# A decoder step's attention: inverse sums turned one place later, the sample's fourth key group, new keys and row turns moved in the plan

## The chip, the core and the metric

The kernel runs on one core of one Trainium2 chip. The metric is the device time of one execution in microseconds (us), the median of several runs. The engines are TensorE (PE; its weight loads are PEld), VectorE (DVE), ScalarE (ACT), GpSimd (POOL) and SyncE (SP), which here issues the DMAs.

## What is computed

One layer of a decoder for a prompt group (1024 tokens, 1 sequence) and a sample group (8 sequences of 8 new tokens, each with 2048 cached keys in 16 pages). The layer is a half-step feed-forward block, three branches on the normed input (sparse attention, a gated recurrence, cross-attention into 256 memory tokens), their gated merge, and a second half-step feed-forward block. The part that matters here:

```python
def sparse_core(q, k_sel, v_sel, valid):
    s = jnp.einsum("bthd,btkhd->bthk", q, k_sel, preferred_element_type=jnp.float32) * (DH_ATT ** -0.5)
    s = jnp.where(valid[:, :, None, :], s, -jnp.inf)
    p = jax.nn.softmax(s, axis=-1).astype(v_sel.dtype)
    o = jnp.einsum("bthk,btkhd->bthd", p, v_sel)

def mem_attend(qm, mk, mv):
    s = jnp.einsum("bthd,bmhd->bthm", qm, mk, preferred_element_type=jnp.float32) * (DH_MEM ** -0.5)
    p = jax.nn.softmax(s, axis=-1).astype(mv.dtype)
    o = jnp.einsum("bthm,bmhd->bthd", p, mv)
```

## The kernel before

The kernel first runs feed-forward 1 and the input projections, then head norms (`keys_and_heads`), then `attention`, whose last steps run into `merge`, then feed-forward 2. Only `attention_plan` (L2802) is touched. It returns a list of entries in one order, and `on_pe`, `on_act` and `on_dve` (L3141, L3322, L3380) each walk that list and issue their share of every entry. So the list is the program order of all three engines. An engine's instruction waits on semaphores, and all that is queued behind it on that engine waits too.

The prompt's work is cut into 48 **doubles**: for each of 4 head pairs, 8 doubles of attention (query blocks of 128 rows in the order 0, 7, 1, 6, 2, 5, 3, 4; a query block i sees 128(i+1) keys, two heads at a time) and 4 of memory attention (two query blocks, one head). The entries of a double d are

- `scores` (L3160): TensorE forms the scores into banks 0 to 3; VectorE reduces them to negative maxima (L3406, or L3410 and L3412 for memory). Scores of d wait until those of d-1 are read: by VectorE's reduction for attention, by ScalarE's exponentials for memory (`scores_read`, L2983).
- `exp` (L3332): ScalarE takes two exponentials with row sums.
- `turn` (L3188): TensorE transposes the probabilities, up to 4 blocks a turn, and ScalarE or VectorE copies the bank out (`evict`, L2995; the even turns of the plan go to ScalarE, the odd ones to VectorE).
- `invert` (L3413): VectorE takes the reciprocals of the sums and spreads them (L3422, memory L3425).
- `inverse` (L3217): TensorE transposes these (L3221) once VectorE has spread them; they are copied out (L3013).
- `values` (L3194): TensorE multiplies the turned probabilities with the values (L3210, L3214) and VectorE scales the product by the turned inverse (L3432).

In step d the order is scores(d), a first place for the sample, values(d-2), a second place, turn(d-1), invert(d-1), exp(d), a third place, and last inverse(d-1). Right behind the scores of steps 8, 20 and 32 ScalarE copies the next head pair's queries (L3310), and behind those of steps 9, 21 and 33 its keys (L3313); there VectorE takes the low parts of both (L3372, L3374).

The sample's work fills the three places. Each of the 8 samples takes six steps: `sc` 0 to 3 are the scores against four groups of four key pages (TensorE L3236 and L3246, copied out by ScalarE at L3355), `sc` 4 those against the 8 new keys, `smax` VectorE's row maximum over all 2056 columns (L3437), `soft` ScalarE's exponential (L3360), `msc` memory scores, `pt` 0 to 4 the turns of the probabilities (L3261, L3263), `pv` the product with the 16 value pages (L3281), `mpt` and `mpv` the same for memory, `ot` and `mot` the turns of the results. All matmuls of the sample go through bank 5, one after another, each behind the copy of the one before (`freed5`).

Turns take the least recently used of banks 4, 7, 1 and 3; in a **wide** step (d mod 12 in 1, 3, 5, 7, over 512 keys) of 4 and 7 alone, as the scores need 1 and 3.

SyncE loads the pages in its own order: three key slots, so that a sample's group 3 goes into the slot of its group 0 and waits for `sc` 0, and the next sample's group 2 waits for `sc` 3 (L3087). The loads of the value pages wait for `pv` and `mpv` of the sample before (L3101).

Behind double 47, `merge` entries 0 to 4 bring in the first pieces of the merge; entries 3 and 4 give TensorE a branch product each (L3590), which waits for GpSimd's low part of the first weight (L3585).

Of the kernel before, what the change touches and what calls it, by code (L numbers as in the profile page):

```python
# [2801 lines left out]
def attention_plan():  # L2802

    doubles = []
    for hp in range(H // 2):  # L2810
        doubles += [("att", i, 2 * hp) for i in (0, 7, 1, 6, 2, 5, 3, 4)] + [("mem", 2 * m, hp) for m in range(4)]
    slots = [
        ([], [], [("sc", 0)]),
        ([("sc", 1)], [], [("sc", 2)]),
        ([("sc", 3)], [], [("sc", 4), ("smax",)]),
        ([], [], [("soft",), ("msc",)]),
        ([("pt", 0), ("pt", 1), ("pt", 2)], [("pt", 3), ("pt", 4)], [("pv",), ("mpt",)]),
        ([("mpv",)], [("ot",)], [("mot",)]),
    ]
    plan = []  # L2820
    turns = 0

    def add(step, *entry):
        nonlocal turns
        turn = None
        if entry[0] in ("turn", "inverse", "pt", "mpt", "ot", "mot"):
            turn = turns
            turns += 1
        plan.append((entry, turn, step))

    def sample(d, place):
        if d < n:
            for e in slots[d % 6][place]:
                add(d, e[0], d // 6, *e[1:])

    n = len(doubles)
    add(0, "queries", 0)
    add(0, "keys", 0)
    for d in range(n + 2):
        if d < n:  # L2840
            add(d, "scores", d)
            following = d // 12 + 1
            if d % 12 == 8 and following < H // 2:
                add(d, "queries", following)
            if d % 12 == 9 and following < H // 2:
                add(d, "keys", following)
        sample(d, 0)
        if 0 <= d - 2 < n:
            add(d, "values", d - 2)
        if n <= d:  # L2850
            add(d, "merge", 2 + 2 * (d - n))
        sample(d, 1)
        if 0 <= d - 1 < n:
            blocks = 2 * (doubles[d - 1][1] + 1) if doubles[d - 1][0] == "att" else 4
            for g in range(0, blocks, 4):
                add(d, "turn", d - 1, g, min(4, blocks - g))
            add(d, "invert", d - 1)
        if d < n:
            add(d, "exp", d)
        sample(d, 2)  # L2860
        if 0 <= d - 1 < n:
            add(d, "inverse", d - 1)
        if d == n - 1:
            add(d, "merge", 0)
            add(d, "merge", 1)
        elif d == n:
            add(d, "merge", 3)
    return doubles, plan

def attention(nc, sem, mem, bank, bank_t, ident, ident16, qT, kT, qmT, mkT, mv, rq, gains, bias, bias_s, rep, I, O, tail, heads):

    doubles, plan = attention_plan()
    n = len(doubles)
    at = AT_X + 8192
# [1052 lines left out]
```

## Time and profile before

| | us |
|---|---|
| median of 3 runs | 2995.3 (2994.06 to 2997.26) |
| the profiled execution's own time | 2986.76 |
| its span, first to last instruction | 2985.2 |
| TensorE busy | 2825.8 (95%) |
| VectorE busy | 2314.8 (78%) |
| ScalarE busy | 1214.3 (41%) |
| GpSimd busy | 1140.7 (38%) |
| mean granted TensorE clock | 0.982 |

### The profile page before, as it was taken

To read this page: it belongs to the slowest core of one execution; us is meant where nothing else is said; L and a number is where in the kernel's file an instruction comes from. 1 tells how busy PE (TensorE), PEld (TensorE's weight loads), DVE (VectorE), ACT (ScalarE), POOL (GpSimd) and SP (SyncE) were. 2 spreads that over 40 slices of the span, in tenths; PEclk is the share of its full clock that TensorE was granted. 3 is DMA by queue.
4 is the path that set the end of the run, shared out by engine and by line. 5 is a ranking of instruction groups with operands and counts; after the bars stand their busy time and mean duration, and the time that the engine had idled before them with its cause. 6 is when DMAs were issued, how large, how long until landed. Compare 5 with 4: busy or idle time off the path is not lost. (4 is left out here: it accounts for less than half of the span.)

```text
span 2985.2 us, 56695 instructions
## 1 busy us (share of the span) xinstructions
PE 2825.8 (95%) x21274; PEld 2679.2 (90%) x21274; DVE 2314.8 (78%) x3773; ACT 1214.3 (41%) x2361; POOL 1140.7 (38%) x808
## 2 busy tenths in 40 slices
PE   6999989999999999999988888889989999899999
PEld 6999989999899999999985666589889999899999
DVE  8888897777758999999985555547378888977776
ACT  5444444444433333234344444421344444443443
POOL 4545545554543331222321000021355555444552
PEclk8999999999999999999998999999999999999999
DMA  4333323332322222322129766734533333233331
GB/s 159 93 93 93 103 75 93 92 93 86 96 70 87 87 87 74 99 57 82 59 89 320 248 228 233 242 118 133 158 93 107 98 87 106 72 101 98 99 96 58
DMA packets 359405, 340.33 MB, mean 114 GB/s; under 512 B 16831, under 2 KB 293666, under 8 KB 359134
## 3 DMA queue, kind: packets, MB, share of 16 engines
q1 hardware_dynamic: 354430, 330.41, 35.7%
q0 software_dynamic: 4128, 4.20, 0.5%
q8 instruction: 171, 2.80, 0.4%
q10 hardware_dynamic: 576, 2.10, 0.2%
q14 instruction: 100, 0.82, 0.1%
HBM read 299.60 MB, written 37.05 MB: 113 GB/s over the span
## 5 line engine op out<-in xcount | busy, mean ns | idle before, releaser
L294 PE MATMUL bank<-op_r_ffn,w_hi 128*128 128x256 f32 (+1 forms) x2992 | 583.2, 293 | 32.0 <-DVE op_r_ffn L275 17.2
L294 PEld LDWEIGHTS bank<-op_r_ffn,w_hi 128*128 128x128 f32 x2992 | 478.1, 192 | 38.7 <-issue 36.1
L294 PE MATMUL bank<-op_r_ffn,w_lo 128*128 128x256 f32 (+1 forms) x1496 | 434.9, 291 | 0.0
L294 PE MATMUL bank<-h_hi,w_hi 128*128 128x362 f32 (+1 forms) x1272 | 422.1, 332 | 6.7 <-ACT qi L2024 2.6
L435 POOL TENSOR_TENSOR w_lo<-sums_ffn,w_hi 128x512 fp32r<-128x512 f32 x214 | 317.6, 1493 | 266.6 <-ACT w_hi L431 266.6
L294 PE MATMUL bank<-h_lo,w_hi 128*128 128x362 f32 (+1 forms) x1272 | 417.9, 329 | 0.0
L294 PE MATMUL bank<-h_hi,w_lo 128*128 128x362 f32 (+1 forms) x1272 | 417.7, 328 | 0.0
L294 PE MATMUL bank<-op_r_ffn,more_hi_ffn 128*128 128x288 f32 (+1 forms) x1936 | 374.8, 291 | 14.4 <-ACT s_ffn L575 5.3
L294 PEld LDWEIGHTS bank<-op_r_ffn,more_hi_ffn 128*128 128x128 f32 x1936 | 306.3, 190 | 18.3 <-issue 9.0
L435 POOL TENSOR_TENSOR more_lo_ffn<-sums_ffn,more_hi_ffn 128x512 fp32r<-128x512 f32 x138 | 205.4, 1496 | 225.9 <-ACT more_hi_ffn L431 225.9
L294 PEld LDWEIGHTS bank<-op_r_ffn,w_lo 128*128 128x128 f32 x1496 | 287.8, 192 | 0.0
L683 DVE SCALAR_TENSOR_TENSOR x<-bank,x 128x576 f32<-128x576 f32 (+1 forms) x352 | 244.5, 713 | 51.9 <-PE bank L294 51.9
L294 PE MATMUL bank<-op_r_ffn,more_lo_ffn 128*128 128x288 f32 (+1 forms) x968 | 279.8, 289 | 0.0
L1747 POOL TENSOR_TENSOR w_lo<-raw,w_hi 128x1024 fp32r<-128x1024 f32 x53 | 129.5, 2442 | 387.1 <-ACT w_hi L1996 387.0
L3585 POOL TENSOR_TENSOR w_lo<-raw,w_hi 128x1024 fp32r<-128x1024 f32 x28 | 69.2, 2478 | 509.3 <-ACT w_hi L3659 509.3
L294 PEld LDWEIGHTS bank<-h_hi,w_hi 128*128 128x128 f32 x1272 | 240.2, 189 | 11.5 <-DVE h_lo L1425 3.6
L294 PE MATMUL bank<-a_hi_ffn,w_hi 128*128 128x288 f32 (+1 forms) x832 | 242.4, 291 | 5.0 <-DVE x L683 2.1
L294 PEld LDWEIGHTS bank<-h_lo,w_hi 128*128 128x128 f32 x1272 | 240.3, 189 | 2.4 <-issue 0.3
L431 ACT CAST w_hi<-sums_ffn 128x512 fp32r<-128x512 f32 x214 | 130.8, 619 | 272.2 <-PE bank L294 163.6
L294 PE MATMUL bank<-a_lo_ffn,w_hi 128*128 128x288 f32 (+1 forms) x832 | 240.4, 289 | 0.0
L294 PE MATMUL bank<-a_hi_ffn,w_lo 128*128 128x288 f32 (+1 forms) x832 | 240.4, 289 | 0.0
L294 PEld LDWEIGHTS bank<-h_hi,w_lo 128*128 128x128 f32 x1272 | 240.0, 189 | 0.0
(434 smaller groups left out, 6995.8 us busy)
## 6 DMA issues: line engine op xcount, KB each, us to landing
raw<-in_w_ffn_in SPq DMA_DIRECT2D x132, 512.0 KB, 3.9
raw_ffn<-in_w_ffn_out SPq DMA_DIRECT2D x88, 512.0 KB, 3.5
v_ring<-in_cache_v SPq DMA_DIRECT2D x128, 256.0 KB, 4.5
raw<-in_w_in SPq DMA_DIRECT2D x53, 512.0 KB, 4.9
raw_ffn<-in_w_ffn_in SPq DMA_DIRECT2D x44, 512.0 KB, 3.8
kt_two<-in_cache_k SPq DMA_DIRECT2D x88, 256.0 KB, 3.5
kept_g<-stage SPq DMA_DIRECT2D x24, 544.0 KB, 3.1
gate<-kept_g SPq DMA_DIRECT2D x24, 544.0 KB, 3.6
```

Of the source, the lines that this page charges most:

```text
L294: mm = pe.matmul(out, left, right, start=(start and i == 0 and j == 0), stop=(stop and i == n - 1 and j == 2))
L431: act.copy(self.ring_hi[(p + self.turned) % self.RING], self.source(p)).then_inc(self.high, 1)
L435: pool.tensor_tensor(self.ring_lo[(p + self.turned) % self.RING], self.source(p), self.ring_hi[(p + self.turned) % self.RING].bitcast(F32) ...
L683: dve.scalar_tensor_tensor(to, self.bank_t[:, b:b + 2, 0:w], 0.5, to, ALU.mult, ALU.add).then_inc(self.x_added, 1)
L1747: pool.tensor_tensor(w_lo[:, n % 3, :], raw[:, n % 3, :], w_hi[:, n % 3, :].bitcast(F32), ALU.subtract).then_inc(low, 1)
L3585: pool.tensor_tensor(w_lo[:, n % 3, :], raw[:, n % 3, :], w_hi[:, n % 3, :].bitcast(F32), ALU.subtract).then_inc(low, 1)
```

## The change

Two edits of the plan. First, `inverse` of a double no longer closes the step behind it but stands right behind the scores of the step after that, so it comes one entry later: scores(d+1) stands before inverse(d-1) instead of behind it. It is still ahead of values(d-1). Second, three of the sample's entries move within its six steps: `sc` 3 from the first place of step 2 to the third, `sc` 4 and `smax` from the third place of step 2 to the first of step 3, and `pt` 0 to 2 from the first place of step 4 (ahead of the values product) to the second, where `pt` 3 and 4 already are. No instruction is added or taken away. The turns keep their order among themselves, and with it the engine that copies each of them; their banks are chosen anew.

```diff
--- before.py
+++ after.py
@@ -2812,9 +2812,9 @@
     slots = [
         ([], [], [("sc", 0)]),
         ([("sc", 1)], [], [("sc", 2)]),
-        ([("sc", 3)], [], [("sc", 4), ("smax",)]),
-        ([], [], [("soft",), ("msc",)]),
-        ([("pt", 0), ("pt", 1), ("pt", 2)], [("pt", 3), ("pt", 4)], [("pv",), ("mpt",)]),
+        ([], [], [("sc", 3)]),
+        ([("sc", 4), ("smax",)], [], [("soft",), ("msc",)]),
+        ([], [("pt", 0), ("pt", 1), ("pt", 2), ("pt", 3), ("pt", 4)], [("pv",), ("mpt",)]),
         ([("mpv",)], [("ot",)], [("mot",)]),
     ]
     plan = []
@@ -2844,6 +2844,8 @@
                 add(d, "queries", following)
             if d % 12 == 9 and following < H // 2:
                 add(d, "keys", following)
+        if 0 <= d - 2 < n:
+            add(d, "inverse", d - 2)
         sample(d, 0)
         if 0 <= d - 2 < n:
             add(d, "values", d - 2)
@@ -2858,8 +2860,6 @@
         if d < n:
             add(d, "exp", d)
         sample(d, 2)
-        if 0 <= d - 1 < n:
-            add(d, "inverse", d - 1)
         if d == n - 1:
             add(d, "merge", 0)
             add(d, "merge", 1)
```

## Rows read from the trace of the kernel before

**Rows 1.** The page's first part: TensorE over the whole span.
```profile
PE 2825.8 (95%) x21274; PEld 2679.2 (90%) x21274; DVE 2314.8 (78%) x3773; ACT 1214.3 (41%) x2361; POOL 1140.7 (38%) x808
```

**Rows 2.** Busy time by engine, attention phase; last: PEclk, DMA share, GB/s.
```profile
1612.00:1953.00 341.00, 281.38 (x3334) 193.26 (x3333) 187.30 (x479) 159.38 (x389) 2.88 (x1) 0.94 0.72 245
```

**Rows 3.** Waits of TensorE in the attention phase: total us, times, longest.
```profile
PE bank L3221 <- DVE inv L3425: 16.6, 9, 2.9
PE bank L3221 <- DVE inv L3422: 11.1, 12, 1.6
PE bank L3236 <- DMA kt_two<-in_cache_k: 10.6, 5, 4.5
PE bank L3261 <- ACT ps L3360: 5.0, 5, 1.0
...
PE bank L3236 <- DMA kt_third<-in_cache_k: 2.9, 2, 1.6
```

**Rows 4.** Timeline of TensorE, doubles 26 to 28: start, us, instruction, idle before.
```profile
1792.40 0.33 PE L3221 MATMUL bank<-ident,inv 128*128 128x128 f32 x1
...
1794.36 0.40 PE L3236 MATMUL bank<-bias_s,rep 64*32 64x512 bf16 x4 [1.07 <-ACT ps L3355]
...
1795.68 0.44 PE L3210 MATMUL bank<-pt,vp 128*64 128x128 f32 x4
1796.05 1.97 PE L3192 MATMUL bank<-ident,pb_odd 128*128 128x128 f32 x16
...
1799.22 0.30 PE L3221 MATMUL bank<-ident,inv 128*128 128x128 f32 x1 [0.91 <-DVE inv L3422]
...
1804.98 0.30 PE L3221 MATMUL bank<-ident,inv 128*128 128x128 f32 x1 [0.99 <-DVE inv L3422]
...
1807.02 2.07 PE L3261 MATMUL bank<-ident,ps 128*128 128x128 f32 x12 [1.02 <-ACT ps L3360]
```

**Rows 5.** The same stretch on VectorE and ScalarE.
```profile
1799.27 2.29 DVE L3437 TENSOR_REDUCE st<-ps 128x1 f32<-128x2056 f32 x1 [0.20 <-ACT ps L3355]
...
1802.55 1.15 DVE L3406 CUSTOM_DVE_ANT_0 pb_odd<-bank,bias,rq 128x896 f32<-128x896 f32 x1
...
1804.79 1.99 ACT L3360 ACTIVATE ps<-ps,st 128x2056 f32<-128x2056 f32 x1
```

**Rows 6.** Timeline of TensorE and VectorE, doubles 32 to 34.
```profile
1834.05 0.33 PE L3221 MATMUL bank<-ident,inv 128*128 128x128 f32 x1
...
1836.57 0.40 PE L3236 MATMUL bank<-bias_s,rep 64*32 64x512 bf16 x4 [1.33 <-DMA kt_third<-in_cache_k]
...
1848.27 0.41 PE L3221 MATMUL bank<-ident,inv 128*128 128x128 f32 x2 [2.94 <-DVE inv L3425]
...
1849.97 2.56 PE L3261 MATMUL bank<-ident,ps 128*128 128x128 f32 x12
...
1845.10 1.22 DVE L3372 TENSOR_TENSOR q_low<-qT,q_high 128x1024 fp32r<-128x1024 f32 x1
```

**Rows 7.** Timeline of SyncE's DMA issues for sample 5 and the next.
```profile
1830.15 1.88 SPq L3054 DMA_DIRECT2D kt_third<-in_cache_k  x4
...
1848.08 1.88 SPq L3054 DMA_DIRECT2D kt_third<-in_cache_k  x4
```

**Rows 8.** Busy time of one stretch in double 28; columns as before.
```profile
1807.00:1810.00 3.00, 2.98 (x20) 2.40 (x20) 1.06 (x4) 0.96 (x4) 0.00 (x0) 0.63 0.69 214
```

**Rows 9.** Timeline of TensorE, first and last sample of eight.
```profile
1629.39 0.62 PE L3236 MATMUL bank<-bias_s,rep 64*32 64x512 bf16 x4 [4.53 <-DMA kt_two<-in_cache_k]
...
1644.66 2.79 PE L3261 MATMUL bank<-ident,ps 128*128 128x128 f32 x12 [1.01 <-ACT ps L3360]
...
1916.61 0.33 PE L3221 MATMUL bank<-ident,inv 128*128 128x128 f32 x1
...
1931.48 1.75 PE L3261 MATMUL bank<-ident,ps 128*128 128x128 f32 x12 [0.95 <-ACT ps L3360]
```

**Rows 10.** Timeline of TensorE where the merge begins.
```profile
1953.35 0.67 PE L294 MATMUL bank<-mo_hi,w_hi 128*128 128x364 f32 x1 [3.92 <-POOL w_lo L3585]
```

## What the change was predicted to do, before it was run

> **What bounds the kernel now.** I read the page's first part, then the busy time by stretch, then TensorE's waits, then the timelines of the places with waits. TensorE is busy 95% of the span, VectorE 78% [rows 1]. In the attention phase it is less: 281.4 of 341 us, with VectorE at 187.3 and ScalarE at 159.4, a mean granted clock of 0.94 and the DMA engines 72% busy [rows 2]. No other engine is full, so the phase is TensorE's stream plus its waits, and only the waits and the clock can give something back. The wait view names them [rows 3]: 16.6 + 11.1 = 27.7 us before `inverse` for VectorE's spread reciprocals, 10.6 + 2.9 = 13.5 us for key pages, 5.0 us before `pt` for the sample's exponential. That is 46.2 us, and each of the three is touched.
>
> In the timeline the waits are not spread evenly. Of each twelve steps, 2 to 4 (the A stretch) and 8 to 10 (the B stretch) hold nearly all. For A of the third head pair, let T be 1792.40, where TensorE has finished `sc` 2. It waits 1.07 before `sc` 3, 0.91 before one inverse, 0.99 before the next, 1.02 before `pt`, which starts at 1807.02, T+14.6 [rows 4]. For B, T is 1834.05; it waits 1.33 for pages, 2.94 before an inverse, and `pt` starts at 1849.97, T+15.9 [rows 6]. These are chains over three engines, so a wait that goes is not a microsecond won. I work out for each stretch when `pt` starts afterwards.
>
> **The fourth key group (`sc` 3).** It now stands behind values and turn, which are 0.44 + 1.97 = 2.4 us [rows 4]. In B TensorE was at it at 1836.57 - 1.33 = T+1.2 and the pages let it go at T+2.5 [rows 6]; it now gets there at T+3.5 (T+1.2 and about 2.3 for its values and turn), 1.0 us behind the pages, so that wait goes. The pages don't come later: SyncE issues group 3 behind `sc` 0 (here at 1830.15), which isn't moved, and the next sample's group 2, which waits for the moved `sc` 3, only at 1848.08, because SyncE is busy issuing other loads before it [rows 7]; `sc` 3 ends near T+4.9 = 1839. Nine microseconds of cover, so I cost that at nothing; were it gone, each microsecond of lateness would be a microsecond at the next sample's `sc` 2.
>
> **Inverse behind the next scores.** TensorE goes straight to the scores. They need the reduction of the double before (for memory doubles its exponentials), and bank 5 isn't theirs. The inverse then waits only if VectorE is more than one `scores` late. Where VectorE copies the inverse out, that copy now stands behind the reduction. In wide steps with only banks 4 and 7, a later turn wants that bank: two reductions of about 1.1 us [rows 5] against 2.5 us of TensorE's own work in step 5; I allow 0.2 us four times, 0.8 us. At the end of step 11 the inverse's wait becomes the scores' wait for the same double's exponentials, so I book nothing there.
>
> **`sc` 4 and `smax` in step 3.** This is the part that costs. `smax` takes 2.29 us of VectorE [rows 5], and it stood ahead of the reduction of scores(3), in VectorE's idle time. It now stands behind it, and behind `smax` are queued the scaling of values(1), the copy of turn(2) and invert(2), for which TensorE waits at inverse(2); ScalarE's `soft` waits for `smax` itself.
>
> The A stretch then, from T. TensorE reaches the end of double 26 without waits: from 1792.40 to 1799.22 are 6.82, less waits 1.07 and 0.91, less about 0.35 for `sc` 4 [rows 4], T+4.5. Scores(27) end at T+6.0 (about 1.5). VectorE: two reductions of 1.15 and the latency, T+8.3; `smax` 2.29 [rows 5], T+10.7. ScalarE: `soft` 1.99 [rows 5] and the latencies, `pt` at T+13.2. VectorE meanwhile scales, copies a turn and inverts, T+12.0; inverse and values(26) end at T+13.1, just in time, so `pt` has nothing else in its way. Against T+14.6 that is 1.4 us, and values(26), 1.1 us at the clock it met, no longer lies behind `pt` 2. Then the clock: the granted clock was 0.63 in 1807 to 1810 [rows 8], and the 12 transposes took 2.07 against about 1.5 at full clock; with their neighbours 1.1 us. Sum 3.6 us at full clock.
>
> The B stretch. Turn ends at T+3.5, `sc` 3 at T+4.9, exponentials of memory double 32 at T+5.1, scores(33) at T+6.2. VectorE: maxima (0.85) T+7.2; two low parts of 1.22 and a little more [rows 6], T+9.6; inverse copy and `smax` T+12.1; scaling and inversion T+12.9. `soft` lets `pt` go at T+14.4, and inverse and values(32) end there too. Against T+15.9 that is 1.5 us, 1.0 for values before `pt` 3, 0.9 for the slow clock behind the 2.94 wait. Sum 3.4 us.
>
> The first sample: pages land at 1629.39 whatever stands before, `pt` at 1644.66 [rows 9]. Values and turn move into that wait, and from scores(3) the A chain is 13.2 - 4.5 = 8.7 us: `sc` 3 ends at 1631.9, `pt` at about 1641. With values 5.0 us in all. The last sample has no low parts; from T = 1916.61 to `pt` at 1931.48 it took 14.9 [rows 9] and by the same steps takes 13.0; with values 2.9 us.
>
> At the tail inverse(47) moves behind the first branch product. TensorE idles there anyway until GpSimd's weight at 1953.35 [rows 10], so the wait before it brings nothing, and the transposes (0.41 in rows 6) now stand in the path: -0.5 us with latency. The turns of `pt` in one place need four banks in a row; copies of 0.4 us against transposes of 0.45 keep up, at nothing.
>
> Sum: 3 x 3.6 + 3 x 3.4 + 5.0 + 2.9 = 28.9; less 0.8 and 0.5, 27.6 us. The unknown is the clock, 3 x 1.1 + 3 x 0.9 + 0.6 = 6.6 us of it. In the new stretches TensorE still waits twice for 1.3 to 1.5 us. I take half back, 3.3: **24 us**. On the profiled execution's 2986.8 that is 2962.5; this one ran 8.5 below the median, and I subtract from the median 2995.3: **2971**.
>
> The granted clock in this trace fell to its lower level after waits of 1.0 us each with work between [rows 4, 8]. The Trainium skill's page "TensorE: Matmul & The Clock Gate", section "HAM oscillation — how this bites in real kernels", ties a fall to one long unbroken idle gap of TensorE. The row disagrees here, since its longest gap was 1.02. By the page the new stretches would run at full clock throughout.
>
> **The rivals.** *Full clock*: no stretch falls to 1.2 GHz. For it: the longest gap left is 1.5 us instead of 2.94. Against it: 1.02 sufficed [rows 4, 8]. 27.6 us, 2968. Chance 0.12.
>
> *Half of it*: only the page waits go, and VectorE holds each inverse for as long as before, since `smax` has moved into its busy time. For it: `smax` is 2.29 us eight times, 18 us in front of what TensorE waits for. Against it: the reduction comes that much earlier, and scores wait on that, not on `smax`. It gives 13.5 less what is lost behind, about 12 us: 2983. Chance 0.19. Here belongs the case that the change doesn't do what it says, the pages coming 1 to 2 us later in the B stretches.
>
> *Nothing*: the chain from `sc` 3 to `pt` takes 1.2 us more than I have it in A, 1.1 in B; VectorE sets the pace and only the first sample gains. Within 6 us of 2995. Chance 0.08.
>
> *Slower*: one chain, in steps 3 and 9. ScalarE's two exponentials (2.1 us) and VectorE's `smax` run side by side in my sum; if the copy of `sc` 4 comes behind the exponentials, `smax` starts 2.1 us later and the latencies and 2.29 add up in series: 4.4 us more, `pt` at T+17.6 instead of 14.6, less 0.7 for values, +2.3 us eight times: 3013. It decides from 12.1 us between `sc` 3 and `pt`; I have 10.0. Against it: in the list `sc` 4 stands ahead of exp. Chance 0.08.
>
> **How the numbers follow.** Forecast 2971 with 0.53, its own range 2963 to 2979 (32 to 16 us; bounds: all clock losses gone and 4 us more, or all kept and 5 less). The range for 8 in 10 takes in full clock and half, leaves the last two rivals out (0.16), and is stretched by 4 for the latencies set by eye: 2958 to 2987. About 0.2% (6 us) is what a measurement of this kernel tells from no change. Faster 0.53 + 0.12 + 0.19 = 0.84, same 0.08, slower 0.08.
>
> **What would show it.** TensorE's wait for key pages before L3236 falls from 13.5 to under 4 us; the waits before L3221 from 27.7 to 12 to 18, all in steps 3, 4 and 10 and at the tail; the wait before L3261 stays at 3 to 6. In doubles 26 to 28 `pt` starts 13.2 us behind the end of `sc` 2, in 32 to 34 14.4. VectorE's `smax` begins right behind a reduction. Busy times stay. The phase from 1612 to the merge shrinks by some 24 us, what lies behind keeps its length. The prediction is wrong if `smax` waits for ScalarE, if `sc` 3 still waits for pages, or if the granted clock of the phase falls below 0.94.

## The result, and the profile after

The changed kernel takes 2955.7 us (median of 4 runs, 2951.3 to 2958.3) where the kernel before took 2994.7 beside it: a ratio of 0.9877, 95% interval 0.986 to 0.9894, or 37 us less by the ratio and 39 by the medians. In the experiments it took 2952.9 against 2990.8 for the kernel before (0.9876, 0.9859 to 0.9894). Medians and ratios leave out the single executions that lie over 1.5% above the fastest of their kernel (3051.9, 3879.8 and, of the kernel before, 6766.4 us). The forecast was 24 us, 2971, with a range that ended at 2958. So the direction was right and the size was not: the gain was half as large again, and the time lies below the range.

The profiled execution took 2958.25 us, its span is 2956.7. First the page's first part, then the busy time by engine of the attention phase, from the first scores to the first branch product of the merge (columns as in [rows 2]):

```profile
PE 2820.5 (95%) x21274; PEld 2677.3 (91%) x21274; DVE 2312.6 (78%) x3773; ACT 1215.4 (41%) x2361; POOL 1140.6 (39%) x808
```

```profile
1615.00:1922.00 307.00, 271.37 (x3331) 186.77 (x3330) 185.01 (x478) 160.63 (x389) 2.75 (x2) 0.97 0.81 272
```

The counts of instructions over the span are those of [rows 1]. The phase holds the work of [rows 2] in 307 us instead of 341: VectorE and ScalarE are as busy as before, TensorE has 10 us less busy time for the same work, because its mean granted clock is 0.97 instead of 0.94, and the rest is waits (how it divides is below). What lies behind the phase keeps its length: 1031.9 and 1030.3 us in two executions of the kernel before, 1034.7 and 1029.8 in two of the changed one. The phase itself fell from 341.2 and 343.2 to 307.0 and 304.9, by 36.2 in the mean. All of the gain lies there.

TensorE's waits in that phase (who waited for whom, total us, times, longest):

```profile
PE bank L294 <- POOL w_lo L3585: 6.5, 1, 6.5
PE bank L3221 <- DVE inv L3422: 5.7, 4, 1.4
PE bank L3221 <- DVE inv L3425: 4.9, 4, 1.3
PE bank L3170 <- ACT pb_odd L3346: 4.8, 4, 1.2
PE bank L3185 <- ACT pb_odd L3346: 3.4, 3, 1.1
...
PE bank L3236 <- DMA kt_two<-in_cache_k: 2.3, 1, 2.3
```

Against [rows 3]: before `inverse` 10.6 us instead of 27.7; for key pages 2.3 instead of 13.5, all of it in the first sample; before `pt` 0.3 instead of 5.0. New are 8.2 us in which scores wait for ScalarE's exponentials of the memory doubles, which used to be hidden in the wait of the inverse ahead of them. All idle time of TensorE in the phase is 307.0 - 271.4 = 35.6 us instead of 341.0 - 281.4 = 59.6: 24 of the 34 us between these two executions. The other 10 are busy time, and the clock accounts for them: 1 minus the granted clock, summed over the microseconds of the phase, is 9.7 us instead of 19.7.

The A stretch of the third head pair, TensorE, then VectorE, then ScalarE (start, us, instruction, idle before). `sc` 2 ends at T = 1777.43.

```profile
1777.43 0.38 PE L3185 MATMUL bank<-k_high,q_high 64*128 64x256 f32 x2
...
1780.50 0.40 PE L3236 MATMUL bank<-bias_s,rep 64*32 64x512 bf16 x4
...
1789.08 0.30 PE L3221 MATMUL bank<-ident,inv 128*128 128x128 f32 x1 [1.43 <-DVE inv L3422]
1789.31 0.66 PE L3210 MATMUL bank<-pt,vp 128*64 128x128 f32 x8
1790.08 1.94 PE L3261 MATMUL bank<-ident,ps 128*128 128x128 f32 x16
```

```profile
1784.44 1.15 DVE L3406 CUSTOM_DVE_ANT_0 pb_odd<-bank,bias,rq 128x896 f32<-128x896 f32 x1
...
1785.51 2.29 DVE L3437 TENSOR_REDUCE st<-ps 128x1 f32<-128x2056 f32 x1
```

```profile
1787.84 2.01 ACT L3360 ACTIVATE ps<-ps,st 128x2056 f32<-128x2056 f32 x1 [1.06 <-DVE st L3437]
```

`sc` 3 starts without a wait, `smax` right behind the second reduction, and one wait of 1.43 is left where [rows 4] show four of about 1.0. `pt` starts at T+12.65, and its 16 transposes take 1.94, where 12 took 2.07 before.

The B stretch, doubles 32 to 34, T = 1814.82:

```profile
1818.26 0.40 PE L3236 MATMUL bank<-bias_s,rep 64*32 64x512 bf16 x4
...
1825.04 1.13 PE L3170 MATMUL bank<-mkT,qmT 128*128 128x256 f32 x4 [1.21 <-ACT pb_odd L3346]
1827.49 0.65 PE L3221 MATMUL bank<-ident,inv 128*128 128x128 f32 x2 [1.33 <-DVE inv L3425]
...
1829.65 2.54 PE L3261 MATMUL bank<-ident,ps 128*128 128x128 f32 x16
```

```profile
1821.93 1.22 DVE L3372 TENSOR_TENSOR q_low<-qT,q_high 128x1024 fp32r<-128x1024 f32 x1
1823.07 1.28 DVE L3374 SCALAR_TENSOR_TENSOR k_low<-kT,gains,k_high 128x1024 fp32r<-128x1024 f32 x1
...
1824.46 2.29 DVE L3437 TENSOR_REDUCE st<-ps 128x1 f32<-128x2056 f32 x1
```

Here two waits follow each other, 1.21 and 1.33, and behind them the granted clock is at its lower level (busy times of two microseconds, the clock is the third number from the end):

```profile
1828.00:1830.00 2.00, 2.00 (x7) 1.54 (x7) 0.92 (x4) 1.34 (x4) 0.00 (x0) 0.50 0.75 229
```

`pt` starts at T+14.83 here, and at T+14.20 in the stretches that keep the full clock.

To read all eight samples at once I took, for each, how long after T the page product `pv` starts:

| pv behind T, us | first sample | A (three) | B (three) | last |
|---|---|---|---|---|
| before, two executions | 26.2, 23.6 | 21.0, 20.4, 21.2; 21.7, 22.6, 23.6 | 20.1, 21.1, 20.8; 20.4, 19.9, 20.4 | 19.0, 19.6 |
| after, two executions | 20.3, 19.1 | 16.2, 16.2, 16.2; 16.2, 16.2, 16.4 | 18.1, 17.0, 18.3; 17.0, 18.3, 17.0 | 15.7, 15.7 |
| gain, mean | 5.2 | 5.6 each | 2.8 each | 3.6 |

5.2 + 3 x 5.6 + 3 x 2.8 + 3.6 = 34.0, and 0.6 each in B (1.8) between `pv` and the next sample's first scores; that is the 36 us. The kernel after is also steadier: its A stretches agree within 0.2 us where those of before differ by 3.2.

### The profile page after: what moved, and what is told of

Its sections match the earlier page's. It is cut to its first block and busy times, and to the rows that moved or that the text cites. A ratio compares the mean times of both kernels' runs of the same rounds, so it can differ in the third digit from the quotient of the medians.

```text
span 2956.7 us, 56695 instructions
## 1 busy us (share of the span) xinstructions
PE 2820.5 (95%) x21274; PEld 2677.3 (91%) x21274; DVE 2312.6 (78%) x3773; ACT 1215.4 (41%) x2361; POOL 1140.6 (39%) x808
## 3 DMA queue, kind: packets, MB, share of 16 engines
q1 hardware_dynamic: 354430, 330.41, 36.2%
## 5 line engine op out<-in xcount | busy, mean ns | idle before, releaser
L294 PE MATMUL bank<-op_r_ffn,w_hi 128*128 128x256 f32 (+1 forms) x2992 | 583.8, 293 | 33.1 <-DVE op_r_ffn L275 17.2
L294 PE MATMUL bank<-op_r_ffn,more_hi_ffn 128*128 128x288 f32 (+1 forms) x1936 | 375.0, 292 | 14.2 <-ACT s_ffn L575 5.4
L294 PEld LDWEIGHTS bank<-op_r_ffn,more_hi_ffn 128*128 128x128 f32 x1936 | 306.6, 190 | 18.1 <-issue 8.6
```

The source lines that it names most:

```text
L294: mm = pe.matmul(out, left, right, start=(start and i == 0 and j == 0), stop=(stop and i == n - 1 and j == 2))
```

## The experiments

"Clock lost" is the sum of 1 minus the granted clock over the microseconds from 1612 to 1925: 18.8 and 20.5 us in two executions of the kernel before, 11.2 and 8.5 in two of the changed kernel. This fixed window ends 28 to 35 us before the phase of the kernel before does, and 3 to 13 us behind that of the changed and the fastest kernels. So a second figure, "over its phase", takes each kernel from its own first scores to its first branch product: 19.7 and 23.1 before, 9.7 and 6.9 after. (The 20.2 and 23.6 in one expectation below are also sums that reach to the end of the phase.)

### Which edit it was: the two halves

The changed kernel once more, beside both halves:

> The changed kernel once more, to size the gain. Theory 1 (all of it lies between the first scores and the first branch product): the phase is 307 us long again, and the kernel is 31 to 37 us faster than the one before, the 39 us between the first medians being scatter of what lies outside. Theory 2 (some 5 us come from behind the merge, where transfers or the clock fall differently): 37 to 41 us faster, and the stretch from the first branch product to the end is at least 3 us shorter than in a second profile of the kernel before.

> The kernel before once more, for a second profile. Theory 1: from the first scores to the first branch product again 341 us, and what lies outside differs from its first profile by as much as the two kernels differ there (2 to 5 us). Theory 2: outside the phase it is within 1 us of its first profile.

They took 2952.9 (median of 4) and 2991.6 us (one execution); phase 304.9 and 343.2, behind it 1029.8 and 1030.3. These are the second executions of the result above. Nothing comes from behind the merge, as theory 1 of the first has it, though the 38 us between the medians are 1 more than it allowed. Outside the phase the two executions of the kernel before differ by 2.8 us, so differences of that size there mean nothing.

The inverses alone:

The edit, against the kernel before:

```diff
+        if 0 <= d - 2 < n:
+            add(d, "inverse", d - 2)
         sample(d, 0)
...
-        if 0 <= d - 1 < n:
-            add(d, "inverse", d - 1)
```

> Only the inverse behind the next scores; the sample's entries stay as before. Theory of the chain (what counts is the path sc 3, sc 4, smax, soft, pt, and the inverse waits are slack on it): the wait for key pages stays near 13 us, smax still stands ahead of the reduction, so pt starts as late as before in steps 2 to 4 (T+14.6) and about 1.2 us earlier in steps 8 to 10; 4 to 8 us faster in all. Theory of the waits (each wait is worth its own length): 20 to 27 us faster.

2988.7 us, ratio 0.9995 (0.9986 to 1.0004): alone this edit brings nothing that the measurement can tell, where the theory of the chain gave it 4 to 8 us. Of TensorE's waits in the phase, two:

```profile
PE bank L3236 <- DMA kt_two<-in_cache_k: 12.1, 6, 5.2
PE bank L3261 <- ACT ps L3360: 7.7, 5, 1.7
```

The inverse waits are down to 4.7 us. In A TensorE only comes sooner to the pages and to `soft`, which end when they did: `pt` starts at T+15.9 in the mean, as before. In B something is won: `pt` starts at T+14.3 instead of 16.1 and `pv` at 18.0 instead of 20.5, 7 us in three stretches. The profiled execution loses these again, 3 in the first sample (`pv` at T+28.0) and 7 in a stall of 4.26 us inside a page product with the lower clock behind it (see the end). Where the other eleven executions lose them is not on record, so why this edit brings nothing alone is explained for A and open for B.

The sample's entries alone:

The edit, against the kernel before:

```diff
-        ([("sc", 3)], [], [("sc", 4), ("smax",)]),
-        ([], [], [("soft",), ("msc",)]),
-        ([("pt", 0), ("pt", 1), ("pt", 2)], [("pt", 3), ("pt", 4)], [("pv",), ("mpt",)]),
+        ([], [], [("sc", 3)]),
+        ([("sc", 4), ("smax",)], [], [("soft",), ("msc",)]),
+        ([], [("pt", 0), ("pt", 1), ("pt", 2), ("pt", 3), ("pt", 4)], [("pv",), ("mpt",)]),
```

> Only the sample's entries moved; the inverse stays at the end of the step. Theory of the chain: page waits gone but for the first, pt about 1 us later than in the changed kernel (T+13.7 in steps 2 to 4, T+15.5 in 8 to 10), the inverse waits as long or longer; 22 to 28 us faster. Theory of the waits: 13.5 for pages and 5.0 for the exponential, 14 to 19 us faster.

2968.7 us (0.993, 0.9914 to 0.9946), 22 us less. Its waits:

```profile
PE bank L3221 <- DVE inv L3425: 19.1, 9, 3.6
PE bank L3221 <- DVE inv L3422: 9.6, 4, 2.4
```

This is the mechanism of the rival "half": with `smax` ahead of the inversion the single waits for inverses grow to 2.4 and 3.6 us. The clock lost stays at 20.5 (21.5 over its phase). The halves add up to 24 us, both together give 38; 14 us are theirs only jointly.

### Which of the sample's entries

Four kernels undo or do one part. Turns ahead of the values again, in the changed kernel:

The edit, against the changed kernel:

```diff
-        ([], [("pt", 0), ("pt", 1), ("pt", 2), ("pt", 3), ("pt", 4)], [("pv",), ("mpt",)]),
+        ([("pt", 0), ("pt", 1), ("pt", 2)], [("pt", 3), ("pt", 4)], [("pv",), ("mpt",)]),
```

> The changed kernel with the turns pt 0 to 2 back ahead of the values product; all else as changed. Theory of the chain: pt starts no earlier (ScalarE's exponential ends at T+12.6 or T+14.1 whatever stands in front), so the values product, 0.66 to 1.0 us, comes to lie behind it: pv starts 0.7 to 1 us later, eight times, 5 to 8 us slower than the changed kernel. Rival (five turns in a row cost as much in waits for banks as they save): within 2 us of the changed kernel.

2964.0 us (0.9908, 0.9882 to 0.9934): 11 us of the gain go, more than the 5 to 8 expected. `pt` starts as early as in the changed kernel (T+12.66 in A), but `pv` 0.7 later in A and 2.2 later in B (T+19.6, 20.5, 19.6). There TensorE now waits a third time, 1.13 us before `pt`, and all three stretches fall to the lower clock, with values between `pt` 2 and `pt` 3 at that clock.

`sc` 4 and `smax` back behind `sc` 3, ahead of the reduction of scores(3):

The edit, against the changed kernel:

```diff
-        ([], [], [("sc", 3)]),
-        ([("sc", 4), ("smax",)], [], [("soft",), ("msc",)]),
+        ([], [], [("sc", 3), ("sc", 4), ("smax",)]),
+        ([], [], [("soft",), ("msc",)]),
```

> The changed kernel with sc 4 and smax one place earlier, right behind sc 3, so that smax stands ahead of the reduction again. If smax behind the reduction is what costs (my prediction's part that costs), pt starts 1 to 2 us earlier and the kernel is 6 to 12 us faster than the changed one. If the chain only trades it for sc 4's wait on ScalarE's copy (0.7 us) and a later reduction: pt 0.6 us later in steps 2 to 4, 1.2 us earlier in 8 to 10, within 4 us of the changed kernel.

2960.5 us (0.9898, 0.9872 to 0.9925), some 7 slower than the changed kernel by the medians. The intervals overlap, but the slowest of eight executions of the changed kernel (2958.3) lies below three of the four here. Neither expectation came: not 6 to 12 faster, and not within 4. The prediction had called the place of `smax` "the part that costs". It is the other way round: ahead of the reduction it costs, since TensorE must then stand for ScalarE's copy of `sc` 3 before `sc` 4 (6.0 us in all), and in A `pt` starts at T+13.6 to 13.8 instead of 12.7.

> The kernel before with one edit: sc 3 moves from the first place of step 2 to the third, ahead of sc 4 and smax, which stay there. Inverses and row turns stay. All moves of the sample's entries together gave 21 us. Theory 1 (the page waits before sc 3 and what follows from them, a pt that comes late and a lower clock, are most of it): page waits fall from 13.5 to under 4 us, 12 to 18 us in all, 2973 to 2979. Theory 2 (it was the place of the row turns and of smax; sc 3 later only moves the wait to the turns, since smax then comes 2.4 us later too): the page waits go, the waits before pt grow by as much, and the time is 2986 to 2991.

The edit, against the kernel before:

```diff
-        ([("sc", 3)], [], [("sc", 4), ("smax",)]),
+        ([], [], [("sc", 3), ("sc", 4), ("smax",)]),
```

2964.9 us (0.9909, 0.989 to 0.9928): this one entry, moved alone, brings 26 of the 38 us, more than the 12 to 18 that theory 1 gave it. Page waits are down to 2.0 us, and its other waits are

```profile
PE bank L3221 <- DVE inv L3425: 17.5, 9, 3.2
PE bank L3236 <- ACT ps L3355: 6.0, 9, 0.7
PE bank L3221 <- DVE inv L3422: 4.4, 4, 1.3
```

Those for attention inverses fell from 11.1 [rows 3] to 4.4, though no inverse was moved: in step 2 `sc` 3 now stands between the turn and the inverse behind it and gives VectorE the time. `pt` starts at T+13.6 to 13.8 in A and 13.7 to 14.7 in B, where it started at 16.0 and 16.1 in the mean. So the late `sc` 3 fills a page wait and an inverse wait with work, and `pt` comes some 2 us earlier. (The profiled execution also has a stall of 3.15 us, shown at the end.)

> The kernel before with one edit: pt 0 to 2 behind the values product instead of ahead of it. Theory 1 (values fill the wait for soft): the waits before pt, 5.0 us, go, and as pt begins no later than values plus itself did, pv comes 0 to 1 us earlier: 2985 to 2990. Theory 2 (the excess of the A stretches is here, because values no longer runs at the lower clock behind pt's wait): 2 us a stretch in A, 2982 or less.

The edit, against the kernel before:

```diff
-        ([("pt", 0), ("pt", 1), ("pt", 2)], [("pt", 3), ("pt", 4)], [("pv",), ("mpt",)]),
+        ([], [("pt", 0), ("pt", 1), ("pt", 2), ("pt", 3), ("pt", 4)], [("pv",), ("mpt",)]),
```

2985.1 us (0.9977, 0.9963 to 0.9991), 5.6 less, at the near end of theory 1. The wait before `pt` falls from 5.0 to 1.6. From the kernel before to the changed one there is now a ladder: 2990.8, with `sc` 3 late 2964.9, with inverses and turns later too 2960.5, with `smax` behind the reduction 2952.9. The intervals of neighbouring rungs overlap from the second on, so the first step is sure and the sizes of the others are not. The order matters: `smax` behind the reduction gains some 7 us as the last step. As long as the inverses stand at the step's end it gains nothing (2964.9 against 2968.7, where the turns are moved too and the intervals overlap), and in B the traces show that it costs: `pv` starts at T+20.0 instead of 17.9 in the mean.

### Is the clock part of it

The four kernels of this part add reader-less transposes or products of the identity, whose results are overwritten, in front of a wait. They do more work and wait as long; only TensorE isn't idle meanwhile.

The edit, against the kernel before, at the entry inverse:

```diff
+                if d % 12 in (1, 2, 7, 8):
+                    for _ in range({1: 7, 2: 7, 7: 5, 8: 22 if d < 36 else 5}[d % 12]):
+                        pe.transpose(tb[:, 3 * P:4 * P], ident[:, :], ident[:, :])
                 pe.wait_ge(spread, d + 1)
```

> The kernel before with TensorE's waits ahead of the inverse filled by transposes of the identity into an unused part of the bank (7, 7, 5 and 22 of them, 0.11 us each), so that it does work that nobody needs where it waited. Theory of the clock (the part of the gain that my chain doesn't give is TensorE's clock, which fell behind these waits): the granted clock of the attention phase rises from 0.94 to 0.97 or more, and the kernel is 4 to 10 us faster than before although it does more. Rival (the clock falls for other reasons, and the waits are harmless): within 2 us or slower.

2987.8 us against 2991.6 (0.998, 0.9965 to 0.9995), and clock lost 11.9 instead of 18.8 and 20.5 (over its phase 13.8 instead of 19.7 and 23.1, a granted clock of 0.96, short of the 0.97 expected). More work is faster by some 4 us, which waits alone can't do. One rival isn't excluded: the stall inside the page product of sample 5, 0.43 and 0.70 us in the two executions of the kernel before, is absent here, which is up to 1 of the 4.

The edit, against the kernel with the sample's entries alone:

```diff
+                for _ in range({2: 17, 8: 26, 11: 7}.get(d % 12, 0)):
+                    pe.transpose(tb[:, 3 * P:4 * P], ident[:, :], ident[:, :])
                 pe.wait_ge(spread, d + 1)
```

> The kernel with the sample's entries moved and the inverses left at the step's end (2968.7 us, clock lost in the phase 20.5 us), with identity transposes ahead of its long inverse waits: 17 ahead of inverse(2) (2.40 us), 26 ahead of inverse(8) (3.58 us), 7 ahead of inverse(11) (1.16 us). Its reader-less transposes fill waits that stay as long as they are. The two edits of the change gave 1.5 and 21 us alone and 37 together, so 15 are theirs only jointly. Theory 1 (a good part of the 15 is the clock: the moved entries lengthen the inverse waits to 2.4 and 3.6, the clock falls behind them, and the move of the inverse takes the waits away): the clock lost falls to 10 to 13, and the kernel is 5 to 8 us faster than without the transposes, 2961 to 2964. Theory 2 (the 15 are the waits alone, 28.7 us in that kernel against 11 in the changed one): the clock lost stays near 20 and the time at 2967 to 2970.

2963.2 us (0.9907, 0.989 to 0.9924) against 2968.7, clock lost 6.6 instead of 20.5 (over its phase 6.8 instead of 21.5). In the trace `pv` comes 1.7 us earlier in A (T+17.0) and 2.8 in B (T+17.2), 13 us in six stretches; the profiled execution gives part back in two stalls, 2.95 and 3.07 us, before page products (see the end), and in the last sample the transposes outlast the wait (pv 1.5 later). So some 5 of the 14 joint microseconds are the clock by the medians, and up to 13 by the offsets. The intervals of the two kernels overlap; the sign is sure from the trace, the size is not, and what the rest of the 14 is stays open.

The edit, against the changed kernel:

```diff
+                for _ in range({2: 10, 8: 9}.get(d % 12, 0)):
+                    pe.transpose(tb[:, 3 * P:4 * P], ident[:, :], ident[:, :])
                 pe.wait_ge(spread, d + 1)
```

> The changed kernel, with identity transposes into the bank of the coming inverse put ahead of the two inverse waits that are left over and over: 10 ahead of inverse(2) in step 4 (its wait is 1.43 us) and 9 ahead of inverse(8) in step 10 (1.33 us). The transposes have no reader. Theory 1 (the waits before these inverses set TensorE to its lower clock in some stretches, which costs 2 to 3 us over the phase): the waits in the record shrink to a few tenths, the clock lost in the phase (the sum of 1 minus the granted clock over its microseconds) falls from 8.5 to 11.2 us to under 8, and the kernel comes out the same or 1 to 3 us faster: 2950 to 2953. Theory 2 (these two waits are too short to matter for the clock): the clock lost stays at 8.5 to 11 and the time is the changed kernel's, 2953 within 2, or up to 2 us longer where a transpose outlasts the wait.

2952.8 us: the changed kernel's time. All three B stretches now have `pt` at T+14.20 and `pv` at T+17.03, the clock lost is 6.8 (5.0 over its phase), but A had nothing left to give (`pv` T+16.2 as before) and the last sample starts `pt` 1.0 late. The clock cost the changed kernel 1.2 us a slow B stretch, half of them being slow: 2 us, which this measurement can't tell from none.

The edit, against the kernel before, at the entry sc:

```diff
+                for _ in range((8 if b else 18) if g == 3 else 0):
+                    pe.matmul(bank[5][:, 0:P], ident[:, :], ident[:, :], start=True, stop=True)
```

> The kernel before with products of the identity with itself into bank 5 ahead of sc 3, which overwrites them: 18 for the first sample, 8 (about 1 us) for each other. They have no reader. Theory 1 (page waits of 1 to 2.6 us set the clock down; so in a second execution of the kernel before the granted clock was 0.52 and 0.63 at 1882 to 1886 behind a page wait of 2.61): the clock lost in the phase falls from 20.2 and 23.6 to 15 to 19 us, and the time by 1 to 4: 2987 to 2990. Theory 2 (it falls for the inverse waits alone): clock lost 20 to 23, and the time is that of the kernel before or up to 2 us more.

2993.6 us (1.0005, 0.999 to 1.0019), no gain, though the clock lost fell to 10.2 (11.3 over its phase), further than theory 1 asked. The trace says why it isn't a clean test: `sc` 3 starts at T+3.9 in A and T+3.5 in B, where the pages let it go at 2.0 to 3.5 and 1.7 to 3.0, so the filling outlasts the pages by about 1 us, seven times, and TensorE waits 5.3 us for ScalarE's copies before it can fill. What the page waits' clock costs by itself in the whole kernel stays open. That it falls behind them is in the traces, behind three of the thirteen page waits outside the first sample in the two executions of the kernel before: 1.85, 1.96 and 2.61 us, and not behind one of 2.30. In the second execution of the kernel before, `sc` 3 of sample 6 waited 2.61 us for pages, and then (its TensorE row, and busy time by stretch)

```profile
1881.16 0.40 PE L3236 MATMUL bank<-bias_s,rep 64*32 64x512 bf16 x4 [2.61 <-DMA kt_two<-in_cache_k]
```

```profile
1882.00:1884.00 2.00, 2.00 (x15) 0.83 (x8) 0.29 (x1) 0.58 (x1) 0.00 (x0) 0.52 0.98 352
1884.00:1886.00 2.00, 2.00 (x13) 2.00 (x12) 0.53 (x1) 0.59 (x2) 0.00 (x0) 0.63 1.11 379
```

This is the most expensive A stretch seen, `pt` at T+17.7 and `pv` at T+23.6.

### What is next in B

The new keys one step later:

The edit, against the changed kernel:

```diff
-            if d % 12 == 9 and following < H // 2:
+            if d % 12 == 10 and following < H // 2:
```

> The changed kernel with the next head pair's key split (ScalarE's copy and VectorE's two low parts, 2.5 us) one step later, in steps 10, 22 and 34. In steps 8 to 10 smax follows the maxima directly, so pt starts at about T+12.3, as for the last sample, which has no split. If nothing of step 10 waits for it: 2 us three times, 5 to 7 us faster than the changed kernel. If the copies of pt wait behind it: within 2 us, with pv as late as before.

2954.3 us (0.9873, 0.9841 to 0.9906), no change. `pt` starts at T+12.3 but `pt` 4 only at 16.1, because the wait moved:

```profile
PE bank L3261 <- DVE inv_t L3013: 5.4, 3, 1.8
```

The low parts now stand ahead of the copy of an inverse whose bank a turn wants. Moving both low parts only moved the queue. Taking one of them out of the queue:

The edit, against the changed kernel, VectorE:

```diff
-    def split_low(dve, hp):
+    def queries_low(dve, hp):
         dve.wait_ge(q_high, hp + 1)
         dve.tensor_tensor(q_lo[:, :], qT[:, hp, 0:SEQ], q_hi[:, :].bitcast(F32), ALU.subtract).then_inc(q_low, 1)
+
+    def split_low(dve, hp):
+        if not hp:
+            queries_low(dve, hp)
         dve.wait_ge(k_high, hp + 1)
...
+            if kind == "exp" and s % 12 == 8 and s < 36:
+                queries_low(dve, s // 12 + 1)
```

> The changed kernel, with VectorE's low part of the next head pair's queries (L3372, 1.22 us) taken out of step 9, where it stands between the maxima of scores(9) and smax, and put behind invert(7) in step 8, where VectorE is idle for 1.9 us. Nothing is added or left out. Theory 1 (in the B stretch the chain maxima, two low parts, smax, soft sets when pt starts): smax starts 1.2 us earlier, pt in doubles 32 to 34 at T+13.0 (full clock) instead of T+14.2, three times, and the wait before inverse(8) falls from 1.33 to about 0.2; 3.6 us and up to 3 more of clock: 2946 to 2950. Theory 2 (the score wait for ScalarE's exponentials of double 9, 1.21 us, sets it): pt comes under 0.5 us earlier and the time is 2951 to 2954.

2947.5 us (0.9848, 0.9831 to 0.9865), 5.4 us under the changed kernel and the fastest kernel here: its slowest execution, 2948.2, is faster than the fastest of eight of the changed kernel, 2951.3. Doubles 32 to 34, VectorE, then TensorE (T = 1806.96):

```profile
1811.23 1.22 DVE L3372 TENSOR_TENSOR q_low<-qT,q_high 128x1024 fp32r<-128x1024 f32 x1
...
1814.08 1.28 DVE L3378 SCALAR_TENSOR_TENSOR k_low<-kT,gains,k_high 128x1024 fp32r<-128x1024 f32 x1
...
1815.47 2.28 DVE L3443 TENSOR_REDUCE st<-ps 128x1 f32<-128x2056 f32 x1
```

```profile
1817.18 1.13 PE L3170 MATMUL bank<-mkT,qmT 128*128 128x256 f32 x4 [1.21 <-ACT pb_odd L3346]
1818.50 0.41 PE L3221 MATMUL bank<-ident,inv 128*128 128x128 f32 x2 [0.19 <-DVE inv L3431]
...
1820.04 1.94 PE L3261 MATMUL bank<-ident,ps 128*128 128x128 f32 x16 [0.26 <-ACT ps L3360]
```

`smax` starts 1.1 us earlier behind T, the wait before the inverse falls from 1.33 to 0.19, `pt` starts at T+13.08 in all three B stretches, and none is slow any more: `pv` at T+15.9 instead of 17.0 or 18.3. The wait for the exponentials (1.21) is still there and didn't hinder it.

The tail, on top of this:

The edit, against the kernel above, ScalarE's part of the merge's first pieces:

```diff
             elif step == 1:
+                high_part(act, 0)
                 split_high(act, 0, 2)
             elif step == 2:
                 split_high(act, 0, 3)
-            elif step == 3:
-                high_part(act, 0)
```

> The kernel before this one, and at the end of the attention phase ScalarE makes the high part of the first merge weight (L3659, 1.0 us) ahead of the third and fourth high part of the first branch, instead of behind them and a turn's copy. GpSimd's low part (2.8 us), for which TensorE waits 6.5 us before the first branch product, can then start 2 to 3 us earlier. Theory 1 (GpSimd's low part is what the first product waits for): that wait falls to 3.5 to 4.5, and the time is 2 to 3 us under the kernel without this edit: 2944 to 2948. Theory 2 (the low parts of the branch, the last of which VectorE ends only at 1923.1, or the DMA of the weight, issued at 1910.9, take its place): under 1 us of it arrives in the merge's length, and the time is that of the kernel without this edit.

2952.7 us (0.9865, 0.9845 to 0.9884): 5 us worse than without it (the intervals overlap; three of the four executions here are slower than all five there). Theory 2 holds, and more. In the record (TensorE at the third of the first products, then VectorE and GpSimd where the merge begins):

```profile
1921.09 0.67 PE L294 MATMUL bank<-mo_hi,w_hi 128*128 128x364 f32 x1 [4.71 <-DVE mo_lo L3769]
```

```profile
1911.83 3.42 DVE L3769 TENSOR_TENSOR mo_lo<-oy,mo_hi 128x1088 fp32r<-128x1088 f32 x1
...
1915.36 2.33 DVE L3431 COPY inv<-stats 128x256 f32<-128x256 f32 x1
```

```profile
1911.75 2.35 POOL L3591 TENSOR_TENSOR w_lo<-raw,w_hi 128x1024 fp32r<-128x1024 f32 x1 [305.84 <-ACT w_hi L3665]
1915.18 4.70 POOL L3591 TENSOR_TENSOR w_lo<-raw,w_hi 128x1024 fp32r<-128x1024 f32 x2 [1.08 <-ACT w_hi L3665]
```

The first product starts earlier (14.5 us behind `pv` of the last sample instead of 17.3), but the low parts that the later ones need come later, and the round of products ends 2.6 us later: `mo_lo` takes 3.42 us beside GpSimd's subtraction where it takes 1.29 alone, and the spread of the inverse 2.33 where it takes 0.29. They end 1.15 and 0.16 us behind GpSimd's instruction (1915.25 against 1914.10, 1917.69 against 1917.53), about their own length or less, as if they ran only behind it. Without the edit one `mo_lo` is held up in the same way (3.44 us, ending 1.15 behind GpSimd's); with it two are, and the spread as well. These 2.6 us are shown; the rest of the 5 isn't.

## Why the prediction came out too small

**The sign and the place were right.** The gain lies in the phase, what lies behind keeps its length, pages no longer hold `sc` 3, `smax` starts right behind a reduction and waits for nothing, `sc` 4 stands ahead of the exponentials (so the slower rival has no ground), busy times stay. At the tail the wait for GpSimd's weight grew from 3.9 to 6.5 and took the place of the inverse's, as worked out, at 0.15 us gained (pv to the merge 17.70, then 17.56) instead of 0.5 lost.

**The A stretch: the step that failed is its price before.** The term 1.4 us came from T+14.6, read off the third head pair. That is the earliest `pt` of the six A stretches in two executions; their mean is T+16.0. In the third pair `sc` 3 could start at T+2.0, in the other five at T+2.5 to 3.5, when their pages came. In four of the six `pt` starts 12.66 or 12.67 us behind the start of `sc` 3. In the two others it starts 14.2 behind it, because TensorE's clock had fallen behind page waits of 1.96 and 2.61. The later pages make 0.8 us of the difference in the mean, the clock 0.5. One row with a random part was taken for all three. Of the 2.0 us that each A stretch brought above the 3.6, 1.3 are this. The chain afterwards was worked out at 13.2 and came at 12.65, another 0.55, from latencies set by eye. The values and clock behind it were right: 2.2 worked out, 2.3 measured (pt to pv 5.8, then 3.5).

**The clock was taken back wrongly.** I took back half of 6.6 us. In A the one wait that is left, 1.43, hardly ever brought the clock down: of 15 A stretches in five executions that have it, 14 have `pv` at T+16.2 to 16.5 and one at 18.1. In B half of the stretches are slow, behind two waits, 1.21 and 1.33, with one `scores` between them. A slow B stretch is 1.2 longer, so half of three cost 1.8, and about 1.5 of the 3.3 taken back had no reason; the two filling runs show that the clock is a real part of the gain and of its joint part. The Trainium skill's page "TensorE: Matmul & The Clock Gate", section "HAM oscillation — how this bites in real kernels", would leave the new stretches at full clock throughout, as their longest idle gap is 1.43: right for A, wrong for B (0.50 at 1828 to 1830). The prediction gave 1.02 as the longest gap of the stretch before; [rows 4] have 1.07, before `sc` 3, which changes nothing in the comparison.

**The B stretch** was worked out at 3.4 and brought 2.8 to `pv`. `pt` moved by 1.6 (16.1, then 14.5 in the mean; 1.5 was predicted); of the 1.9 for values and clock behind it only 1.2 came, half of the stretches being slow. But another 0.6 each came between `pv` and the next sample, which I had at nothing. Before it varied (11.3 to 12.3), afterwards it is 11.1 each time. 0.2 of it is in all of them; what varied goes with short stalls inside the page product (0.27 us in the second head pair of one execution, 0.43 and 0.70 in the third of both), which the two executions of the changed kernel don't have. So this part of the gain was luck, as far as the forecast goes.

**The small terms.** The first sample gave 5.2 (5.0 predicted), the last 3.6 (2.9). The 0.8 us for inverse copies behind reductions in wide steps was not paid: `sc` 0 to T is 7.2 and 7.9 us before and after. The waits before `pt` were to stay at 3 to 6 and went, as values now ends just when `soft` does; those before `inverse` fell to 10.6, below the 12 to 18 given.

**The price of `smax`.** "This is the part that costs" was right in the kernel with the entries alone (inverse waits of 2.4 and 3.6) and wrong with the inverses moved. Terms that stand on the same queue can't be priced one by one: measured alone, `sc` 3 late is worth 26 us, the turns 5.6 and the inverses 2 that can't be told from none, and the some 7 of `smax` exist only with all of them.

**What the 12 us too little are made of.** By the offsets: the price of A before 3 x 1.3 = 3.9, its chain afterwards 3 x 0.55 = 1.7, 3 x 0.6 = 1.8 between `pv` and the next sample, 1.5 of clock taken back without reason, 0.8 for the wide steps, 0.7 at the tail, 0.9 for the first and last sample, together 11. The price of A before is the largest single term, and no one term is all of it.

**The range.** Its lower end took in 4 us for latencies and the full clock but no spread of what stood before. A base that varies by 3 us from stretch to stretch had to widen it: with the means of the A stretches the sum is 24 + 3 x 1.3 = 28, and with the full clock 31.

## What to carry to other kernels

Price a stretch that repeats from all its instances, and where they differ ask which wait is random (here the DMA of the key pages, up to 2.6 us): removing it removes its spread too. When several edits touch one in-order queue, work out their order on that queue together; an entry that costs by itself can gain once the entry behind it has moved. And look for work that sits in a chain only by habit: one subtraction of 1.2 us taken out of a busy place brought 5.4 us, where moving its neighbours (the next keys' copy and both low parts) one step later brought nothing.

## What the runs showed of the hardware

- **TensorE's clock fell behind short waits, and not each time.** Behind one wait of 1.43 us in 1 stretch of 15, behind two of 1.21 and 1.33 in 3 of 6, behind page waits of 1.85, 1.96 and 2.61 but not behind one of 2.30. Filling waits with useless transposes cut the clock lost over the phase from 19.7 and 23.1 to 13.8 us in the kernel before and made it some 4 us faster (ratio 0.998, 0.9965 to 0.9995).
- **VectorE and GpSimd hold each other up.** A subtraction of 1.29 us took 3.42, a copy of 0.29 took 2.33 beside GpSimd's subtractions, and each ended only behind GpSimd's, by 1.15 and 0.16 us. The other way round, a GpSimd subtraction took 3.41 us instead of 2.35, with the last 1.2 us of a VectorE subtraction inside it (kernel without the tail edit). The Trainium skill's page "GPSIMD Engine Reference", section "1. Specifications", says that GpSimd contends with VectorE instructions that have two inputs in SBUF, which the subtraction has, or that run in a two-port mode; whether the copy does, no run here shows.
- **Stalls in which no engine works.** In the profiled execution with `sc` 3 late, TensorE stands in the middle of a page product, with VectorE and ScalarE idle too:

```profile
1843.57 0.87 PE L3281 MATMUL bank<-v_ring,pts 128*32 128x128 f32 x21 [3.15 <-issue]
```

  Stalls of 2.1 to 4.3 us before or in a page product stand in the profiled executions of five of the kernels here. They are not all at different places: in three of the five the stall is in sample 5 behind the 107th of 128 matmuls, 4.26 us with the inverses alone, 3.15 with `sc` 3 late, 2.07 with the turns alone. At that same matmul TensorE idles for 0.43 and 0.70 us in the kernel before and for 0.63 in the one with the sample's entries alone, and not at all in the changed kernel (two executions) and the six made from it. Behind the stall shown, the granted clock was 0.57 and 0.58 for four microseconds. What they wait for, the traces don't show, and no run here tests whether they are a part of the 14 joint microseconds. With the clock behind it the longest cost 7 us, and by so much a single profiled execution can mislead.
